# Low parts of a weight block moved to GpSimd, and a re-ordered VectorE loop, in a three-pass float32 block kernel

## The reference

```
def _ffn_sublayer(h, mod, g_pre, g_post, w_in, w_out):
    shift, scale, gate = mod
    u = _modulate(_rmsnorm(h, g_pre), shift, scale)
    a, b = jnp.split(u @ w_in, 2, axis=-1)
    y = (jax.nn.silu(a) * b) @ w_out
    return h + MACARON_W * gate * _rmsnorm(y, g_post)
```

## Time and profile before

| | us |
|---|---|
| median of 3 runs (2318.19 to 2322.07) | 2321.14 |
| the profiled execution's own time | 2317.03 |
| its span | 2315.2 |
| TensorE busy | 2245.9 (97%) |
| VectorE busy | 1461.7 (63%) |
| ScalarE busy | 1010.6 (44%) |
| GpSimd busy | 34.6 (1%), 35 instructions |

### The profile page before, as it was taken

The page is one execution under the profiler, slowest core; times in us unless marked ns, Lnnn a source line. Parts: engine busy times, 40 slices in busy tenths (PEclk is TensorE's granted clock), DMA queues, the critical chain, the costliest instruction groups (busy, mean ns, idle before and its releaser), DMA issues.

```text
span 2315.2 us, 39422 instructions
## 1 busy us (share of the span) xinstructions
PE 2245.9 (97%) x14069; PEld 1911.3 (83%) x14069; DVE 1461.7 (63%) x2074; ACT 1010.6 (44%) x1468; POOL 34.6 (1%) x35
## 2 busy tenths in 40 slices
PE   7999999999999999999999999999899999999998
PEld 5888888788777888888788888788799989889897
DVE  4874577766668872777532234866764577857765
ACT  4322224544455332225422224545554456455554
POOL 0000000000000000000000000000000000000000
PEclk9999999999999999999999999999999999999999
DMA  9664555322134653655333335432256644215321
GB/s 338 191 187 125 159 173 173 119 65 71 40 91 121 190 179 112 178 159 151 91 86 95 109 84 161 122 108 76 93 160 172 178 140 146 84 38 165 101 74 55
DMA packets 399398, 298.66 MB, mean 129 GB/s; under 512 B 13342, under 2 KB 361252, under 8 KB 399140
## 3 DMA queue, kind: packets, MB, share of 16 engines
q1 hardware_dynamic: 365322, 231.58, 34.2%
q10 hardware_dynamic: 33946, 65.35, 8.7%
HBM read 295.84 MB, written 1.06 MB: 128 GB/s over the span
## 4 chain that ended last, share of the span: by engine, by line
PE 81%; DVE 10%; issue 3%; ACT 3%; DMA 2%; SPq 1%; DVEq 0%; ACTq 0%; POOL 0%; POOLq 0%
PE banks L1089 24%; PE banks L1091 23%; PE banks L1090 23%; PE banks L1356 2%; ACT wh L1856 1%; DVE wl L2532 1%; DMA wraw<-in_ffn_w_in 1%; DVE uR L2466 1%; DVE yT L2652 1%; DVE yT L2454 1%; PE banks L1189 1%; PE banks L1306 1%; PE banks L1298 1%; PE banks L1220 1%; PE banks L1037 1%
## 5 line engine op out<-in xcount | busy, mean ns | idle before, releaser
L1089 PE MATMUL banks<-uR,wh 128*128 128x512 f32 (+1 forms) x2368 | 827.7, 350 | 27.5 <-DVE uR L2466 22.1
L1090 PE MATMUL banks<-uR,wh 128*128 128x512 f32 (+1 forms) x2368 | 811.2, 343 | 0.0
L1091 PE MATMUL banks<-uR,wl 128*128 128x512 f32 (+1 forms) x2368 | 811.1, 343 | 0.0
L2532 DVE TENSOR_TENSOR wl<-wraw,wh 128x2048 fp32r<-128x2048 f32 (+2 forms) x202 | 423.8, 2098 | 324.1 <-ACTq L1783 313.6
L1856 ACT ACTIVATE wh<-wraw 128x2048 fp32r<-128x2048 f32 (+4 forms) x208 | 367.0, 1765 | 428.1 <-PE banks L1091 373.1
L1089 PEld LDWEIGHTS banks<-uR,wh 128*128 128x128 f32 x2368 | 449.0, 190 | 102.0 <-issue 24.7
L1091 PEld LDWEIGHTS banks<-uR,wl 128*128 128x128 f32 x2368 | 449.1, 190 | 52.9
L1090 PEld LDWEIGHTS banks<-uR,wh 128*128 128x128 f32 x2368 | 449.6, 190 | 49.2 <-issue 0.5
L1089 PE MATMUL banks<-gR,wh 128*128 128x512 f32 (+1 forms) x704 | 256.8, 365 | 2.0 <-DVEq L2378 1.8
L1091 PE MATMUL banks<-gR,wl 128*128 128x512 f32 (+1 forms) x704 | 255.3, 363 | 0.0
L1090 PE MATMUL banks<-gR,wh 128*128 128x512 f32 (+1 forms) x704 | 255.2, 363 | 0.0
(11 more groups left out here) (346 smaller groups left out, 2377.3 us busy)
## 6 DMA issues: line engine op xcount, KB each, us to landing
wraw<-in_ffn_w_in SPq DMA_DIRECT2D x176, 512.0 KB, 5.2
ada_buf<-in_ada_w ACTq DMA_DIRECT2D x24, 1280.0 KB, 6.0
wraw<-in_w_in SPq DMA_DIRECT2D x56, 512.0 KB, 4.7
wraw<-in_ffn_w_out SPq DMA_DIRECT2D x64, 384.0 KB, 4.2
wraw<-in_ffn_w_out SPq DMA_DIRECT2D x64, 320.0 KB, 4.5
ada_buf<-in_ada_w ACTq DMA_DIRECT2D x24, 768.0 KB, 4.5
wraw<-in_da_w_in SPq DMA_DIRECT2D x24, 512.0 KB, 4.5
wraw<-in_na_w_in SPq DMA_DIRECT2D x24, 512.0 KB, 4.2
```

Of the source, the lines that this page charges most:

```text
L1089: mm(o, a[0], b[0], start=first, stop=False)
L1090: mm(o, a[0], b[1], start=False, stop=False)
L1091: return mm(o, a[1], b[0], start=False, stop=last)
L2532: do(V.tensor_tensor(wl[:, s, 0:n], wraw[:, s, 0:n], wh[:, s, 0:n].bitcast(F32), ALU.subtract), w_lo)
```

## The change

GpSimd makes both column halves of the low part of the second weight block (`low_columns`), right behind its second `root` of the passage. VectorE no longer has those instructions; it waits for GpSimd's semaphore `low_half` ahead of the chunks' loop and behind it, and raises `w_half` and `w_lo` itself. VectorE's loop is written in another order. TensorE does 3 instead of 5 of the 8 chunks of a modulation product ahead of the second spread, where there is one.

```diff
@@ postnorm (TensorE)
                 if n == 2:
-                    fill_mul(st, 0, o, range(5))
+                    fill_mul(st, 0, o, range(3))
                 else:
                     spare(psum[7], 8)
                 spread(T - c0, 4 + c0 // P)
                 if n == 2:
-                    fill_mul(st, 0, o, range(5, DC))
+                    fill_mul(st, 0, o, range(3, DC))
@@ GpSimd
+            def low_columns(b, j):
+
+                hi, lo, raw = [x[:, b % 2, :].rearrange("p (k n) -> p k n", k=DC)[:, :, j * P:j * P + P] for x in (wh, wl, wraw)]
+                nc.gpsimd.tensor_tensor(lo, raw, hi.bitcast(F32), ALU.subtract).then_inc(low_half, 1)
...
                     root((T - c0) // P)
                     root((T - c0) // P, 4 + c0 // P)
+                    b = FIRST_BLOCK[run[run.index(st) + 1]] + 1
+                    pool.wait_ge(n1_half, cols.up())
+                    low_columns(b, 0)
+                    pool.wait_ge(w_hi, b + 1)
+                    low_columns(b, 1)
@@ residual (VectorE), ahead of the chunks
-                else:
-                    dve.wait_ge(n1_half, tl["cols"].up())
-                    rest_columns(b + 1, 0, ks=slice(0, DC // 2))
...
-                else:
-                    rest_columns(b + 1, 0, w_half, ks=slice(DC // 2, DC))
-                b += 1
...
                 scale(0)
+                scale(1)
                 add(0)
-                scale(1)
-                if feed and c0:
-                    dve.wait_ge(n1_half, tl["cols"].up())
-                    rest_columns(b, 0, w_half)
+                add(1)
                 rs, free2 = product(small)
                 normed(0)
-                add(1)
+                scale(2)
                 normed(1)
-                scale(2)
                 add(2)
+                dve.wait_ge(low_half, tl["pool"].up())
+                dve.sem_inc(w_half, 1)
                 for k in range(DC):
+                    if k + 3 < DC:
+                        scale(k + 3)
                     low(to, streams, k)
+                    if k + 3 < DC:
+                        add(k + 3)
                     if k + 2 < DC:
                         normed(k + 2)
...
-                    if k + 3 < DC:
-                        scale(k + 3)
-                        add(k + 3)
...
-                dve.wait_ge(w_hi, tl["split"].up())
-                rest_columns(b, 1, w_lo)
+                tl["split"].up()
+                dve.wait_ge(low_half, tl["pool"].up())
+                dve.sem_inc(w_lo, 1)
```

More of the change, by code:

```diff
@@ L367, in build @@
         root_ready = sem("root_ready")
+        low_half = sem("low_half")
         n_ready = sem("n_ready")
@@ L684, in chunks_of @@
             return [dst[:, k - k0, :] for dst, k0, k1 in parts for k in range(k0, k1)]
-        SIZES = []
+        SIZES, FIRST_BLOCK = [], {}
         for st in run:
+            FIRST_BLOCK[st] = len(SIZES)
             if st.startswith("ffn"):
@@ L2339, in root @@
                                         ALU.pow).then_inc(root_ready, 1)
+            def low_columns(b, j):
+                hi, lo, raw = [x[:, b % 2, :].rearrange("p (k n) -> p k n", k=DC)[:, :, j * P:j * P + P] for x in (wh, wl, wraw)]
+                nc.gpsimd.tensor_tensor(lo, raw, hi.bitcast(F32), ALU.subtract).then_inc(low_half, 1)
+            cols = Tally()
             root(TT, 4)
@@ L2369, in _ @@
             tl = {k: Tally() for k in ("root", "wide", "silu", "exp", "pv", "aa", "sq", "sq2", "copy", "gy", "split", "uh", "gh", "ada", "half", "sums",
-                                       "n", "tail", "cols", "landed0", "landed1")}
+                                       "n", "pool", "tail", "cols", "landed0", "landed1")}
             V = nc.vector
```

## The result

| | before | after |
|---|---|---|
| median of 5 runs each | 2318.28 us (2316.34 to 2322.07) | 2332.92 us (2331.98 to 2335.23) |
| ratio | 1 | 1.0057, 95% interval 1.0046 to 1.0067 |
| profiled execution: span | 2315.2 us | 2331.1 us |
| granted TensorE clock, mean | 0.997 | 0.990 |

The changed kernel is slower by 0.57%, some 13 us. (The ratio is worked out from all runs of both kernels, not from the two medians, which differ by 14.6 us here.) A second measurement in another set of runs gave the same ratio (experiment 11).

The account below looks back on a forecast made before the run. TensorE was taken to wait on VectorE's loop in six passages. 15.0 us lost to GpSimd's subtractions and 9.7 won made +5.3; 2321.1 + 5.3 = 2326.4 us, range 2311 to 2336.

Parts of the forecast that it names:

- likeliest case: Whole kernel: GpSimd subtractions of 2.0 to 2.7 us hold VectorE's adds; 2323 to 2330 us, chance 0.37.
- reads hold reads: SBUF: while GpSimd's subtraction reads, VectorE's two-operand reads wait, and the reverse; 2.5 us lost in passage 1, 15.0 in all.
- What bounds the kernel: Six passages: TensorE waits for VectorE's loop, whose period is 2.52 us against 2.07 of matmuls per chunk.
- One for one: Passage ends: whatever moves `low(0)` or the loop's period moves the end of the passage by the same amount.
- What the change wins, 9.7 us: VectorE, six passages: subtractions gone ahead of the chunks and fewer stalls; 1.2 to 2.1 us a passage, sum 9.7.
- How long a subtraction takes, 2.3 us: GpSimd: one 128x1024 subtraction was estimated at 2.3 us, its two operands passing one after the other.
- The bounds of 1.2 and 5.4: GpSimd subtraction: limits from VectorE's 1.22 us and a 4.4 times ratio; the sum would be -4 or +42 us.
- nothing is held: VectorE's adds beside GpSimd's reads lose only hundredths; sum -9.7 us, 2311.4 us, chance 0.22.
- Who goes first: Passage 1: `add(0)` waits 1.95 us, then `add(1)` passes before GpSimd's second subtraction; `add(2)` waits 0.6.
- GpSimd comes first: Between `add(0)` and `add(1)` waiting GpSimd gets the path, `add(1)` waits a whole subtraction; +13.8 us, 2334.9, chance 0.17.
- The clock: TensorE: longer idle time might lower its granted clock, making it slower than any case above; no size given.
- The moved fillings, nothing: TensorE between the spreads: 3 chunks of filling instead of 5 ahead of the second spread, priced at nothing.

Follow-up runs that it names:

- experiment 11: The changed kernel unaltered, measured again against the kernel before in another set of runs: 2332.49 us, ratio 1.0057.
- experiment 3: The changed kernel with GpSimd's twelve subtractions replaced by writes of zeros to the same places: 2309.37 us, ratio 0.9951 to the kernel before.
- experiment 6: The changed kernel with VectorE steps that read PSUM put between the first two additions: 2325.42 us, ratio 1.0028 to the kernel before.
- experiment 5: The changed kernel with 15 more unread multiplications by the identity on TensorE at the end of the filling: 2329.58 us, ratio 1.0036 to the kernel before.
- experiment 4: The kernel before with only the fillings divided anew, 3 chunks ahead of the second spread instead of 5: 2319.23 us, ratio 0.9998.

## Why the prediction was right, and where not

Slower was forecast, by 5.3 us, with 2311 to 2336 as the range; 2332.9 lies in it, at the place of a rival (2334.9), and outside the 2323 to 2330 of the likeliest case. The direction was right for the reason given, that reads hold reads; that the number is in the range is due to the rival at its end.

- *What bounds the kernel.* Held in the main. In eleven kernels the time moved with `low(7)`, to within 3 us in eight of them. "One for one" was too strong: TensorE's end doesn't follow `low(7)` at a fixed distance, and with its own clock and order taken in the time is met better (the table's fourth column).
- *What the change wins, 9.7 us.* Held in size: with the hold taken away it is 11.4 by the times and 10.2 by TensorE's end (experiment 3), of which 7.2 and 5.8 are the order's. In its parts it was less exact. `scale(0)` did move as said, and `normed(0)` came 0.5 us earlier in passage 1; but `low(0)`, which was to come 0.6 us earlier, came only 0.2 earlier, since it now waited 0.51 us for ScalarE. The prediction had said that ScalarE's step for chunk 0 moves with `normed(0)`. It doesn't, since ScalarE has a copy of `gs` to do first, and that waits for TensorE's filling. Experiment 3, passage 1 (`normed(0)` had started at 423.27):

```profile
424.28 0.28 ACT L1818 ACTIVATE gs<-banks 128x128 f32<-128x128 f32 x1 [3.81 <-PE banks L884]
424.67 0.60 ACT L1848 ACTIVATE uR<-yT,mod,coefA 128x256 fp32r<-128x256 f32 x1
```

```profile
426.86 0.69 DVE L2479 TENSOR_TENSOR uR<-yT,uR 128x512 fp32r<-128x512 f32 x1 [0.51 <-ACT yT L1850]
```

- *How long a subtraction takes, 2.3 us.* Held: 2.35 us for the first of a pair. The bounds of 1.2 and 5.4 were not needed.
- *That reads hold reads.* Held, against "nothing is held" (chance 0.22): experiments 3 and 6.
- *Who goes first.* This is the step that failed. The forecast let `add(0)` and `add(1)` both through ahead of GpSimd's second subtraction, on the strength of one tie in the trace before, where the two engines had started together. On the chip the waiting engine goes next: behind `add(0)` GpSimd had its turn and `add(1)` waited a whole subtraction. In passage 1 `low(0)` was to be 1.9 us later (2.5 lost, 0.6 won) and was 3.3 us later; the end of the passage was to be 0.9 us later, and `low(7)` was 2.5 later. The rival "GpSimd comes first" had this, with +13.8 us and a chance of 0.17. A tie says who wins when both arrive; it says nothing of an engine that has been waiting while the other worked. The row showed the first, and the second was wanted.

  By the Trainium skill (SBUF — State Buffer, § SBUF: two separate sides), of a VectorE instruction with two SBUF inputs and a GpSimd instruction that reads SBUF, the one that starts first has the shared ports for its whole length. For the long subtraction the trace agrees (`add(0)` was through 0.54 us after it ended). Who goes next after a wait that section doesn't say. The rows say the one that waited: GpSimd's second subtraction starts at 424.43, before `add(0)` is through at 425.01, and it goes ahead of `add(1)`. On that hung 8.5 us, the distance from the forecast to the rival.
- *The clock.* Named as a thing that would make the forecast wrong, and given no price: at 1.22 us of idle time no row showed it. At 3.9 to 4.8 us the granted clock fell in all six passages (0.86 to 0.95 by stretch), which cost about 3 us by the rows and 5 by the times (experiment 5).
- *Does it add up?* The rival and the clock together would be +17, and +13.2 was measured. By the rows the rest is the size of the holds: `low(0)` stands 3.5, 2.8, 3.5, 3.5, 3.5 and 4.1 us behind experiment 3's in the six passages, 20.9 us in all, where the rival had 23.5 (13.8 and the 9.7 won). With experiment 3's -10.2 and 3.0 us between `low(7)` and TensorE's end that makes the +13.7 of the table. What stays open are the 3.1 and 2.1 us by which experiments 5 and 9 were faster than their rows say.
- *The moved fillings, nothing.* Held by themselves (experiment 4). With `normed(0)` early they are no longer quite free: in experiment 3 the `gs` copy comes 6.54 us behind the variance row, in the kernel before 6.32, and it is this copy that `low(0)` ends up waiting for.

## What to carry to other kernels

Work that reads SBUF on GpSimd isn't free for being off VectorE: before moving it, look for VectorE steps with two SBUF operands in the stretch where it will run, and count the rest of the running GpSimd instruction for the first such step, and a whole one for each that stands back to back with it while GpSimd has more queued. If it must be there, cut it into short instructions and put steps that read PSUM between. And test the two halves of a change alone: here the order was worth 7 us and was hidden under the other half.

## What the runs showed of the hardware that I had not expected

- GpSimd and VectorE take turns by instruction. Two additions in a row of VectorE waited 1.9 us and then 2.2 us, with one GpSimd subtraction between them.
- The hold doesn't need two tensors read on GpSimd's side: a copy does it, a fill with zeros doesn't.
- A GpSimd subtraction of 128x1024 takes 2.35 us, a copy 1.03 and a fill 0.95 (two in a row take 1.84). The subtraction of half the size took 1.27 us at the shortest.
- The length of TensorE's gap alone doesn't decide whether the clock falls. In passage 2 of the kernel before it was 2.23 us and the stretch kept 1.00; in experiment 4 it was 2.24 us, and the same stretch had 0.95. In experiment 6 some matmuls behind the 3.24 us gap of passage 1 take 0.63 us instead of 0.39, and none of the first behind the longer one of passage 2 does:

```profile
430.36 0.47 PE L1091 MATMUL banks<-uR,wh 128*128 128x512 f32 x1 [3.24 <-DVE uR L2479]
...
431.56 0.63 PE L1092 MATMUL banks<-uR,wh 128*128 128x512 f32 x1
...
716.24 0.47 PE L1091 MATMUL banks<-uR,wh 128*128 128x512 f32 x1 [3.76 <-DVE uR L2479]
717.01 0.40 PE L1091 MATMUL banks<-uR,wh 128*128 128x512 f32 x1
```
